# A three-block model on one core: order in the last attention steps and at the forget heads, a second chunk stage begun tile by tile, and changes at the route and its refill

## The chip, the core and the metric

One Trainium2 chip; the kernel runs on one of its cores. TensorE (PE) multiplies matrices into eight PSUM banks, VectorE (DVE) and ScalarE (ACT) read them and work on rows, GpSimd (POOL) takes a few products and the broadcast rows, and SyncE (SP) issues the transfers of all weights. Each engine runs its own instructions in order and waits on semaphores. The metric is the device time in microseconds (us) of one execution.

## What is computed

Two layers of hybrid attention (`first_block`), then one layer of a second model (`second_block`), all in float32, for 256 tokens of width 1024. Cut to what matters here:

```python
# first block, each of 2 layers
h = split_cols((x * (1 + scale) + shift) @ w_in)
o_dsa = attention over the top 64 keys, chosen by an index score
o_fox = softmax(q k / 8 + cum_t - cum_s) v      # cum: running sum of log_sigmoid(forget logit)
o_nsa = gated sum of compressed, selected and window attention
x = layer_norm(ALPHA * x + (1 + gate) * ((mix * silu(gate_cols)) @ w_out))
# second block
streams q, k, v, decays g and weights beta, for the context (s=0) and the latents (s=1)
gdn_chunked: per chunk of 64 tokens, head and direction
    A = strict(kb k^T * decay);  T = (1 + A)^-1;  u = T (v beta);  w = T (kb exp(gcum))
    then a scan over 4 chunks: v_new = u - w state;  o = q state + attn v_new;  state = ...
h = h + gt1 * (concat(chunk_mlp, gdn_out) @ w_out)
aff = softmax(rms_norm(h) ... @ w_router + b_router)
each of 16 experts takes its 32 best tokens: silu(x w_gate) * (x w_up) @ w_down, added back by gate
out = rms_norm(h + gt2 * experts)
```

## The kernel before, in words

**The stream.** All weights pass as 148 units of 2 MB in the order of use (`unit_order`). SyncE issues them one after the other; each waits until the unit that held its place before has been used, by the event of the last product that read it (`slots`, and the loop at L517 to L547). There are 4 places in a ring, and 6 more that come free only when the second block ends with them (the slots of `more` and `pieces`). Of those, the three of `pieces` are filled by two transfers of 1 MB, all else by one of 2 MB. From unit 52 on the units are the experts': four of gate and up, then two of down, for each expert. Unit 54 takes a place that the first products of the second chunk stage have read (`G_mm`), 55 waits for the last state product but one, 56 and 57 for the last mixed rows, 58 and 59 for the output products `y2_mm`, 60 for the last half of the residual (`h_lat`), 61 for the last growth row (`grow_mm`), and 62 for the first expert product (`gu_mm` 0, 0), whose ring slot it refills. 65 waits for the first down product.

**Attention** (`pe_attend`, L932). Eleven pairs of heads pass through a pipeline: scores at step m, transposes of the probabilities of m-2 (`pe_probT`), the product with V of m-3 (`pe_pv`). ACT and DVE turn scores into probabilities and copy the transposes. Between them PE works off products of other kinds. When the pairs are through (steps 11 and 12), the output product's first five chunks are worked, one half of the columns at each step (`pe_y`, ranges 0 to 5), between `pe_pv` and `pe_probT`.

**Forget heads** (`pe_layer`, L990; `v_layer`). After column group 4 PE turns (transposes) block 7, whose rows are H's, then blocks 8 to 10, which are forget heads and need the running sums. DVE finds the top 64 of the first tile in 8 rounds (`v_top`), then copies the running sums (`v_fox_cum`), then H (`v_h` 4), then copies block 7 (`v_turn` 7, four operations), adds the compress offsets (`v_blocks`), copies block 9, ropes q and copies block 11. The second half of the compress product (`pe_cmp1`, bank 3) needs block 11's copy, and behind it stands the product of column group 5 for tile 1.

**Chunk stages** (`pe_chunks`, `v_chunks`, `a_chunks`), s=0 for the context and s=1 for the latents, each of two tiles of 128 tokens with banks 0 to 3 and 4 to 7. DVE spreads g and beta over 512 columns (`v_spread`); PE transposes k and v (`k_mm`, `v_mm`), sums the decays (`R_mm`, `BR_mm`), multiplies k by k and q (`G_mm`). `v_head` copies V with a factor, makes the differences (`diff`), ACT their exponential (`decay`), DVE masks them (`M`) and, for the latents, the attention part; level 0 gives `TT` from `Y`, and `T` from the transposed `Y` (`Y_mm` 0). Five levels follow, with small 64 by 64 products, DVE, ACT and POOL in turn. In each part tile 0 goes before tile 1. The end of a stage makes U and W (`U_mm`, `W_mm`). The context's states are worked between the latents' levels. `pe_recur` is the scan of the latents.

**Route** (`pe_route`, `v_route`, `a_route`). The residual is transposed and multiplied by the router while ACT sums the squares of each tile in one operation of 1024; root, reciprocal, softmax; PE transposes the affinities; two growth rows (`pe_grow`) follow on PE while DVE finds the 32 best tokens of each expert in four rounds of 8; PE transposes the places (`place_mm`) and gathers the first four experts' rows (`pe_gather_first`).

**Experts** (`pe_experts`). For each: gate and up products, transposes, down products, and the add of the last expert's result into banks 0 to 3. The last unit comes in two halves; the four last adds stand behind its second half. `v_final` and `a_final` norm the rows and write them.

## Time and profile before

| | us |
|---|---|
| median of 3 runs | 1230.63 (1230.54 to 1231.61) |
| profiled execution: time | 1233.2 |
| profiled execution: span | 1231.4 |
| PE busy | 1060.6 (86%) |
| DVE busy | 432.9 (35%) |
| ACT busy | 236.2 (19%) |
| mean granted clock of PE | 0.937 |

```profile
PE   5999999999999999999998989899776676666667
DVE  0128645423865536255146764421000000100001
PEclk9999999999999999899998989799887888988879
DMA  9963348443346964014221004899999999999996
GB/s 384 414 244 137 138 145 333 146 156 133 130 148 254 429 263 154 1 69 159 82 104 70 4 30 177 340 427 429 430 428 432 429 428 433 428 430 430 430 430 287
PE 58%; DMA 29%; DVE 6%; issue 3%; ACT 2%; SPq 1%; POOL 0%; DVEq 0%; ACTq 0%; POOLq 0%
```

The first five lines cut the span into 40 slices of 30.8 us: busy tenths of PE and DVE, the clock granted to PE in tenths of full speed, the busy share of the transfer engines and what they moved. The last line is the chain of work that ended last, by engine. Attention is in slices 0 to 14, the streams to 18, the context's chunk stage to 20, the latents' to 23, mixing and route to 25, the experts from there.

### The profile page before, as it was taken

How to read it: one execution, taken by the hardware profiler on the slowest of the kernel's cores; microseconds unless marked ns; L12 is line 12 of the kernel's file. 1: busy time of each engine (PE TensorE's matmuls, PEld its weight loads, DVE VectorE, ACT ScalarE, POOL GpSimd, SP SyncE). 2: the span in 40 equal slices, each digit the busy share in tenths (PEclk: the TensorE clock that was granted, in tenths of full speed). 3: DMA queues.
4: the chain of work that ended last, by engine and by line, in shares of the span. 5: the costliest groups of instructions: out<-in, count | busy, mean ns of one | idle time of the engine just before them, and what ended most of it. 6: DMA issues, size and time to landing. Idle time of an engine off the chain costs nothing.

```text
span 1231.4 us, 17863 instructions
## 1 busy us (share of the span) xinstructions
PE 1060.6 (86%) x7574; PEld 572.8 (47%) x7574; DVE 432.9 (35%) x1026; ACT 236.2 (19%) x584; POOL 54.3 (4%) x69
## 2 busy tenths in 40 slices
PE   5999999999999999999998989899776676666667
PEld 2345764444576447985667875432211111111112
DVE  0128645423865536255146764421000000100001
ACT  0012134111313504434112341210000000000002
POOL 0101000000100000000212310000000000000000
PEclk9999999999999999899998989799887888988879
DMA  9963348443346964014221004899999999999996
GB/s 384 414 244 137 138 145 333 146 156 133 130 148 254 429 263 154 1 69 159 82 104 70 4 30 177 340 427 429 430 428 432 429 428 433 428 430 430 430 430 287
DMA packets 28014, 323.66 MB, mean 263 GB/s; under 512 B 3248, under 2 KB 3376, under 8 KB 5792
## 3 DMA queue, kind: packets, MB, share of 16 engines
q1 hardware_dynamic: 25904, 314.18, 62.2%
q0 software_dynamic: 2032, 8.35, 2.0%
q8 instruction: 60, 0.98, 0.3%
q14 instruction: 18, 0.15, 0.0%
HBM read 321.47 MB, written 1.05 MB: 262 GB/s over the span
## 4 chain that ended last, share of the span: by engine, by line
PE 58%; DMA 29%; DVE 6%; issue 3%; ACT 2%; SPq 1%; POOL 0%; DVEq 0%; ACTq 0%; POOLq 0%
PE banks L638 48%; DMA zuv_to_Kt<-in_stream 16%; DMA ring<-in_stream 7%; DMA scr_qk<-in_stream 6%; PE banks L649 3%; PE banks L2160 1%; PE banks L901 1%; SPq L545 1%; PE banks L887 1%; PE banks L922 1%; PE banks L884 1%; PE banks L788 1%; DVE KC L1237 0%; PE banks L892 0%; DVE scr_qk L2495 0%
## 5 line engine op out<-in xcount | busy, mean ns | idle before, releaser
L638 PE MATMUL banks<-ring,uT 128*128 128x512 f32 (+1 forms) x512 | 224.8, 593 | 6.0 <-DVE uT L1104 2.9
L638 PEld LDWEIGHTS banks<-ring,uT 128*128 128x128 f32 x512 | 95.7, 191 | 119.6 <-issue 114.0
L638 PE MATMUL banks<-scr_qk 64*64 64x64 f32 (+4 forms) x2368 | 116.8, 276 | 23.0 <-DMA scr_qk<-in_stream 18.1
L638 PE MATMUL banks<-ring,scr_qk 128*32 128x512 f32 (+1 forms) x496 | 86.0, 650 | 28.1 <-DMA ring<-in_stream 27.7
L638 PEld LDWEIGHTS banks<-scr_qk 64*64 64x64 f32 (+3 forms) x2368 | 87.0, 138 | 48.1 <-issue 33.7
L638 PE MATMUL banks<-ring,UWK 128*32 128x512 f32 (+1 forms) x336 | 86.1, 788 | 16.1 <-DMA ring<-in_stream 9.1
L2705 DVE SCALAR_TENSOR_TENSOR UWK<-UWK,banks 128x256 f32<-128x256 f32 x16 | 6.7, 421 | 261.4 <-ACT UWK L2972 261.4
L2972 ACT ACTIVATE UWK<-banks 128x256 f32<-128x256 f32 x16 | 6.1, 383 | 359.3 <-PE banks L638 359.3
L638 PE MATMUL banks<-UWK,ring 128*128 128x256 f32 x320 | 72.1, 385 | 0.0
L638 PEld LDWEIGHTS banks<-UWK,ring 128*128 128x128 f32 x320 | 61.7, 194 | 9.4 <-issue 1.0
L2160 PE MATMUL banks<-UWK 128*128 128x512 f32 x128 | 64.9, 632 | 0.0
L638 PEld LDWEIGHTS banks<-ring,scr_qk 128*32 128x32 f32 (+1 forms) x496 | 24.5, 125 | 77.1 <-issue 45.6
L649 PE MATMUL banks<-ring,KC 128*32 128x512 f32 x384 | 49.0, 636 | 12.5 <-DMA ring<-in_stream 12.5
L638 PE MATMUL banks<-uT,ring 128*128 128x256 f32 x256 | 59.2, 392 | 0.0
L638 PEld LDWEIGHTS banks<-ring,UWK 128*32 128x32 f32 (+1 forms) x336 | 26.9, 150 | 60.5 <-issue 48.7
L638 PEld LDWEIGHTS banks<-uT,ring 128*128 128x128 f32 x256 | 50.1, 199 | 7.1
L2713 DVE TENSOR_TENSOR UWK<-banks,grow 128x512 f32<-128x512 f32 x16 | 11.1, 692 | 107.2 <-PE banks L638 107.2
L1605 ACT ACTIVATE probs<-banks,mx 128x128 f32<-128x128 f32 x88 | 36.6, 418 | 42.0 <-DVE mx L1374 37.9
L2160 PEld LDWEIGHTS banks<-UWK 128*128 128x128 f32 x128 | 22.7, 197 | 46.3 <-issue 46.3
L1126 DVE COPY H<-banks 128x512 f32<-128x512 f32 (+1 forms) x12 | 8.2, 681 | 84.8 <-PE banks L638 84.7
L638 PE MATMUL banks<-const,scr_qk 64*64 64x64 f32 (+1 forms) x208 | 15.9, 384 | 22.6 <-DMA misc<-in_stream 20.3
L638 PE MATMUL banks<-Vt_to_O,UWK 128*64 128x128 f32 (+1 forms) x208 | 25.9, 557 | 8.2 <-ACT UWK L2980 4.6
(374 smaller groups left out, 1217.0 us busy)
## 6 DMA issues: line engine op xcount, KB each, us to landing
ring<-in_stream SPq DMA_DIRECT2D x94, 2048.0 KB, 14.2
scr_qk<-in_stream SPq DMA_DIRECT2D x11, 2048.0 KB, 38.8
Vt_to_O<-in_stream SPq DMA_DIRECT2D x11, 2048.0 KB, 38.5
zuv_to_Kt<-in_stream SPq DMA_DIRECT2D x10, 2048.0 KB, 38.9
scr_qk<-in_stream SPq DMA_DIRECT2D x11, 1024.0 KB, 41.3
wide<-in_stream SPq DMA_DIRECT2D x10, 1024.0 KB, 39.0
const<-in_stream SPq DMA_DIRECT2D x10, 1024.0 KB, 39.0
misc<-in_stream SPq DMA_DIRECT2D x10, 1024.0 KB, 39.9
```

Of the source, the lines that this page charges most:

```text
L545: sp.dma_start(held(slot[k]), A["stream"][k, :, :]).then_inc(*tick(f"arrived{slot[k]}", by=16))
L638: return pe.matmul(o, a, b, start=start, stop=stop)
L649: ins = pe.matmul(bank[b][32 * j:32 * j + 32, :], window[:, j * (DCH // 4) + k, lo:lo + 32], w[:, j * (DCH // 4) + k, :], start=(n, k) == ...
L788: ins = pe.transpose(bank[b][0:rows, (2 * m + t) * P:(2 * m + t + 1) * P], f(t), ident)
L884: pe.matmul(bank[b + s][:, 0:P], q[:, 0:P], k[:, 0:P], start=True, stop=False)
L887: pe.matmul(bank[b + s][:, P:384], q[:, P:SEQ], k[:, :], start=False, stop=False)
L901: ins = pe.transpose(bank[4 + s][:, i * P:(i + 1) * P], probs[:, m % 3, s, i * P:(i + 1) * P], ident)
L922: pe.matmul(bank[6][HD * s:HD * s + HD, 0:SEQ], H[:, 0, v:v + HD], probT[:, m % 2, s, 0:SEQ], start=first and kind != "slc", stop=False)
L1126: dve.tensor_copy(H[:, 1, AT[cg]:AT[cg] + WIDTHS[cg]], bank[b][:, 0:WIDTHS[cg]]).then_inc(*drain(b, "h", l, cg, 1))
L1605: ins = act.activation(probs[:, i, s, lo:hi], bank[b + s][:, lo:hi], ACT.Exp, bias=mx[:, i, s, t:t + 1], accum_out=den[:, i, s, t:t + 1])
L2160: ins = pe.matmul(bank[2 * t + h], PgT[:, t, :], ye[:, h, 0:512], start=e == 0, stop=e == EXPERTS - 1)
L2713: dve.tensor_tensor(ye[:, 0, 0:512], bank[4], grow[:, 0:512], ALU.mult).then_inc(*drain(4, "ye", e, 0))
```

## The change

At steps 11 and 12 of attention the partial output product stands before `pe_pv`. In each attention layer the running sums of the forget heads are copied after six of the eight rounds of the top 64, and PE turns blocks 8, 9, 10 before 7. In the latents' chunk stage PE works tile 0's decays, first products and transposes before tile 1's, with k's transposes in bank 2 (6) and not 0 (4); DVE spreads tile 0 between the U and W copies of the context's stage and interleaves the tiles; ACT copies V and loads its exponential ahead. The stream's unit 54 waits for the last V transposes. At the route ACT squares tile 1 by halves, before the second logit copy, and DVE adds the two sums; PE has two products of 512 and 256 columns whose result is not used, each behind a round of the top-k. Unit 62 is filled in two halves, the first when half of the first expert product is done. Of the last adds, one stands before the wait for the last half. The context's stage keeps its order.

```diff
@@ -66,6 +66,7 @@
 ONCE = SPLIT[2]
+PLACES = RING + EXTRA + 1
@@ -193,7 +194,7 @@
         past = seen.setdefault(b, [])
-        parts[b] = parts.get(b, 0) + (2 if b in SPLIT and k < len(order) - 1 else 1)
+        parts[b] = parts.get(b, 0) + (2 if (b in SPLIT or k == first + PLACES) and k < len(order) - 1 else 1)
         use.append(parts[b])
@@ -525,10 +526,13 @@
                     sp.dma_start(par[:, P_FIRST:P_COLS], A["params"][:, P_FIRST:P_COLS]).then_inc(*tick("params_in", "params", 1, by=16))
-                if before[k] is not None:
+                again = units[before[k]] == ("gu_mm", 0, 0) if before[k] is not None else False
+                if again:
+                    sp.wait_ge(*at("gu_half"))
+                elif before[k] is not None:
                     sp.wait_ge(*at(*units[before[k]]))
                 elif slot[k] == RING:
-                    sp.wait_ge(*at("G_mm", 1, 1))
+                    sp.wait_ge(*at("v_mm", 1, 1))
                 elif slot[k] == SPLIT[0]:
@@ -537,8 +541,10 @@
                     sp.wait_ge(*at("mix2", 1, 1))
-                if k == len(units) - 1 or slot[k] in SPLIT:
+                if k == len(units) - 1 or slot[k] in SPLIT or again:
                     for i, half in enumerate(halves(slot[k])):
+                        if again and i:
+                            sp.wait_ge(*at(*units[before[k]]))
                         sem = "arrived_last" if (k, i) == (len(units) - 1, 1) else f"arrived{slot[k]}"
@@ -934,6 +940,12 @@
                     pe_scores(pe, l, m)
+                if m == NPAIR:
+                    w_out += [take(pe)]
+                    pe_y(pe, l, 0, 0, w_out, range(0, 5))
+                if m == NPAIR + 1:
+                    w_out += [take(pe)]
+                    pe_y(pe, l, 0, 1, w_out, range(0, 5))
                 if m >= 3:
@@ -947,12 +959,6 @@
                             pe_mod_rows(pe, n)
-                if m == NPAIR:
-                    w_out += [take(pe)]
-                    pe_y(pe, l, 0, 0, w_out, range(0, 5))
-                if m == NPAIR + 1:
-                    w_out += [take(pe)]
-                    pe_y(pe, l, 0, 1, w_out, range(0, 5))
                 if 2 <= m < NPAIR + 2:
@@ -1011,7 +1017,7 @@
                 if cg == 4:
-                    for n in (7, 8, 9, 10):
+                    for n in (8, 9, 10, 7):
                         pe_turn(pe, l, n)
@@ -1502,8 +1508,9 @@
             v_index(dve, l)
-            v_top(dve, 0, P, TOPK // 8)
+            v_top(dve, 0, P, TOPK // 8 - 2)
             v_fox_cum(dve, l)
+            v_top(dve, 0, P, 2)
             v_h(dve, l, 4)
@@ -1804,50 +1811,72 @@
+        def pe_kv_T(pe, s, t):
+            g = TILES * s + t
+            pe.wait_ge(*at("k_ready", s))
+            for b, lo, event in ((4 * t + (2 if s else 0), 0, "k_mm"), (4 * t + 1, H2, "v_mm")):
+                pe.wait_ge(*free(b))
+                for h in range(H2):
+                    ins = pe.transpose(bank[b][:, h * P:(h + 1) * P], KVT[:, lo + h, g * P:(g + 1) * P], ident)
+                ins.then_inc(*fill(b, event, s, t))
+        def pe_decays(pe, s, t):
...
+        def pe_first_products(pe, s, t):
...
+        def pe_first_Y(pe, s, t):
...
+            if s:
+                for t in range(TILES):
+                    pe_decays(pe, 1, t)
+                    pe_first_products(pe, 1, t)
+                    if t:
+                        pe_first_Y(pe, 1, 0)
+                    pe_kv_T(pe, 1, t)
+                pe_first_Y(pe, 1, 1)
+            else:
+                for t in range(TILES):
+                    pe_kv_T(pe, 0, t)
+                for t in range(TILES):
+                    pe_decays(pe, 0, t)
+                for t in range(TILES):
+                    pe_first_products(pe, 0, t)
             if s == 0:
...
                 pe_zuv(pe, zw, 2, 1, 5)
+                for t in range(TILES):
+                    pe_first_Y(pe, 0, t)
             for n in range(LEVELS):
...
+                for t in range(TILES) if n else ():
                     pe.wait_ge(*free(4 * t + 1))
...
+                    pe.wait_ge(*at("T", s, t, n - 1))
+                    ins = small64(pe, 4 * t + 1, scr[:, t, M_, :], scr[:, t, T_, :], t)
                     ins.then_inc(*fill(4 * t + 1, "Y_mm", s, t, n))
@@ -2071,6 +2100,10 @@
             pe_grow(pe, 1)
+            pe.wait_ge(*at("O", 3, 0))
+            for n, width in ((2, 512), (3, 256)):
+                pe.wait_ge(*at("top", n))
+                mm(pe, bank[6][:, 0:width], ident, resid[:, 0, 0:width], True, True)
             pe.wait_ge(*at("place"))
@@ -2118,6 +2151,8 @@
                                  w[:, :, j * 256:(j + 1) * 256], k == 0, k == DCH - 1)
+                    if (e, i, kk) == (0, 0, 0):
+                        ins.then_inc(*tick("half_used", "gu_half"))
                 ins.then_inc(*fill(6, "gu_mm", e, i))
@@ -2132,6 +2167,15 @@
                 ins.then_inc(*fill(7, "hT_mm", e))
+            def add(e, h, tiles=range(TILES)):
@@ -2142,6 +2186,7 @@
                         if final and h:
+                            add(e, 0, (0,))
                             pe.wait_ge(K.sem("arrived_last"), 16)
@@ -2194,8 +2230,8 @@
                 down(e)
-            for h in range(2):
-                add(EXPERTS - 1, h)
+            add(EXPERTS - 1, 0, (1,))
+            add(EXPERTS - 1, 1)
@@ -2394,52 +2430,78 @@
+                v_diff(dve, s, t)
+            for t in range(TILES):
+                v_first_mask(dve, s, t)
+            v_lat_norm(dve)
+            for t in range(TILES):
+                v_first_TT(dve, s, t)
+            for t in range(TILES):
+                v_first_T(dve, s, t)
+        def v_head_latent(dve):
+            v_diff(dve, 1, 0)
+            v_spread(dve, 1, 1)
+            v_first_mask(dve, 1, 0)
+            v_diff(dve, 1, 1)
+            v_attn(dve, 0)
+            v_first_TT(dve, 1, 0)
+            v_first_mask(dve, 1, 1)
+            v_first_T(dve, 1, 0)
+            v_attn(dve, 1)
+            v_first_TT(dve, 1, 1)
+            v_first_T(dve, 1, 1)
...
+        def v_attn(dve, t):
@@ -2498,22 +2560,22 @@
             if s:
-                for t in range(TILES):
-                    v_spread(dve, 1, t)
-            v_head(dve, s)
-            if s == 0:
-                v_lat_norm(dve)
+                v_head_latent(dve)
+            else:
+                v_head(dve, 0)
             for n in range(LEVELS):
...
                     v_Vnew(dve, 0, n, 1, 0).then_inc(*drain(0, "Vnew", 0, n))
-                if n < LEVELS - 1:
+                if 0 < n < LEVELS - 1:
                     v_level(dve, s, n)
-                else:
+                elif n:
                     for t in range(TILES):
                         dve.wait_ge(*at("Y_mm", s, t, n))
+                        if s:
+                            dve.wait_ge(*at("Vt", 1, t))
                         v_weigh(dve, s, t, AT_, Vt, beta, "bV")
@@ -2541,6 +2603,8 @@
                 dve.tensor_copy(WT[:, t, 4:8, :].rearrange("p i d -> p (i d)"), bank[4 * t + 3][:, :]).then_inc(*drain(4 * t + 3, "W", s, t, 1))
+                if s == t == 0:
+                    v_spread(dve, 1, 0)
@@ -2609,6 +2673,8 @@
             v_fT(dve, 1)
+            dve.wait_ge(*at("ssq_h", 2))
+            dve.tensor_tensor(ssq[:, 1:2], ssq[:, 1:2], ssq[:, 2:3], ALU.add).then_inc(*tick("vector_step", "ssq_sum"))
@@ -2616,9 +2682,9 @@
         def v_route(dve):
-            dve.wait_ge(*at("route_mm"))
             dve.wait_ge(*at("rs_h"))
             inverse(dve, rs2[:, 0:TILES], "rs_row")
+            dve.wait_ge(*at("route_mm"))
             for t in range(TILES):
@@ -2643,7 +2709,7 @@
                 src = w if n else first
-                dve.max(t8[0:EXPERTS, :], src).then_inc(*tick("vector_step"))
+                dve.max(t8[0:EXPERTS, :], src).then_inc(*tick("vector_step", "top", n))
                 dve.wait_ge(*last("vector_step"))
@@ -2852,15 +2918,30 @@
         def a_chunks(act, s):
-            for t in range(TILES):
+            def copy_k(t, b):
                 act.wait_ge(*at("k_mm", s, t))
-                if s:
+                act.activation(Kt[:, t, :, :].rearrange("p h d -> p (h d)"), bank[b][:, :], ACT.Copy).then_inc(*drain(b, "Kt", s, t))
+            def decays(t):
+                act.wait_ge(*at("diff", s, t))
+                act.activation(scr[:, t, M_, :], scr[:, t, M_, :], ACT.Exp).then_inc(*tick("scalar_step", "decay", s, t))
+            if s:
+                act.activation(lowest, C("ones")[:, 0:1], ACT.Exp).then_inc(*tick("scalar_step"))
+                for t in range(TILES):
+                    decays(t)
                     act.wait_ge(*at("KG", 0, t))
                     act.wait_ge(*at("bK", 0, t))
-                act.activation(Kt[:, t, :, :].rearrange("p h d -> p (h d)"), bank[4 * t][:, :], ACT.Copy).then_inc(*drain(4 * t, "Kt", s, t))
-            for t in range(TILES):
-                act.wait_ge(*at("diff", s, t))
-                act.activation(scr[:, t, M_, :], scr[:, t, M_, :], ACT.Exp).then_inc(*tick("scalar_step", "decay", s, t))
+                    copy_k(t, 4 * t + 2)
+                    act.wait_ge(*at("v_mm", 1, t))
+                    act.wait_ge(*at("bV", 0, t))
+                    act.activation(Vt[:, t, :, :].rearrange("p h d -> p (h d)"), bank[4 * t + 1][:, :], ACT.Copy,
+                                   scale=0.5).then_inc(*drain(4 * t + 1, "Vt", 1, t))
+            else:
+                for t in range(TILES):
+                    copy_k(t, 4 * t)
+                for t in range(TILES):
+                    decays(t)
             if s == 0:
@@ -2928,16 +3009,28 @@
         def a_route(act):
-            for t in range(TILES):
+            def square(i, x):
+                act.activation(uwk[:, 0:x.shape[-1]], x, ACT.Square, accum_out=ssq[:, i:i + 1]).then_inc(*tick("scalar_step", "ssq_h", i))
+                act.wait_ge(*last("scalar_step"))
+            def copy(t):
                 b = 2 * t + 1
...
                                ACT.Copy).then_inc(*drain(b, "fT", t, 1))
-                for half in range(2):
-                    act.wait_ge(*at("h_lat", t, half))
-                act.activation(uwk[:, 0:D], resid[:, t, :], ACT.Square, accum_out=ssq[:, t:t + 1]).then_inc(*tick("scalar_step"))
-                act.wait_ge(*last("scalar_step"))
+            copy(0)
+            for half in range(2):
+                act.wait_ge(*at("h_lat", 0, half))
+            square(0, resid[:, 0, :])
+            act.wait_ge(*at("h_lat", 1, 0))
+            square(1, resid[:, 1, 0:512])
+            act.wait_ge(*at("h_lat", 1, 1))
+            square(2, resid[:, 1, 512:D])
+            act.wait_ge(*at("ssq_sum"))
             root(act, rs2[:, 0:TILES], ssq[:, 0:TILES], D, "rs_h")
+            copy(1)
             act.activation(lowest, C("ones")[:, 0:1], ACT.Exp).then_inc(*tick("scalar_step"))
...
```

## Rows read from the trace of the kernel before

**Rows 1.** Stretches: length, busy us of each engine, PE's clock, DMA share, GB/s.
```profile
785.00:794.00 9.00, 6.19 (x27) 4.16 (x30) 5.14 (x14) 0.91 (x2) 0.00 (x0) 0.52 1.01 425
794.00:796.00 2.00, 2.00 (x20) 1.09 (x12) 1.10 (x2) 0.00 (x0) 0.00 (x0) 1.00 0.15 57
796.00:798.00 2.00, 2.00 (x19) 0.45 (x17) 0.00 (x0) 0.91 (x2) 0.00 (x0) 1.00 1.01 254
798.00:800.00 2.00, 2.00 (x24) 1.28 (x24) 0.80 (x2) 0.00 (x0) 0.00 (x0) 1.00 0.94 401
...
800.00:900.00 100.00, 86.30 (x594) 28.81 (x590) 13.96 (x26) 8.43 (x19) 0.53 (x1) 0.91 1.01 429
```
**Rows 2.** Timeline of SyncE's issues: start, us, what, [idle before and releaser].
```profile
770.46 4.64 SPq L545 DMA_DIRECT2D ring<-in_stream  x2
...
795.16 3.26 SPq L545 DMA_DIRECT2D ring<-in_stream  x2
...
809.62 0.33 SPq L545 DMA_DIRECT2D Vt_to_O<-in_stream  x1
```
**Rows 3.** Timeline of PE, end of attention in layer 0.
```profile
210.00 0.65 PE L922 MATMUL banks<-H 128*64 128x256 f32 x4 [0.74 <-DVE H L1396]
...
210.80 4.56 PE L638 MATMUL banks<-ring,uT 128*128 128x512 f32 x10
```
**Rows 4.** Timeline of PE, end of attention in layer 1.
```profile
433.30 0.65 PE L922 MATMUL banks<-H 128*64 128x256 f32 x4 [0.74 <-DVE H L1396]
...
434.74 4.56 PE L638 MATMUL banks<-ring,uT 128*128 128x512 f32 x10 [0.57 <-DMA ring<-in_stream]
```
**Rows 5.** Timeline of PE, forget heads and compress, layer 0, then layer 1.
```profile
110.07 0.63 PE L788 MATMUL banks<-const,H 128*128 128x128 f32 x4 [1.08 <-DVE wide L1207]
110.53 1.47 PE L788 MATMUL banks<-const,wide 128*66 128x128 f32 x12
...
121.61 2.05 PE L638 MATMUL banks<-probs,w 128*64 128x30 f32 x32 [0.29 <-DVE TB L1237]
...
123.59 6.28 PE L638 MATMUL banks<-ring,uT 128*128 128x448 f32 x16
...
322.98 0.63 PE L788 MATMUL banks<-const,H 128*128 128x128 f32 x4 [0.90 <-issue]
...
336.62 7.80 PE L638 MATMUL banks<-ring,uT 128*128 128x448 f32 x16
```
**Rows 6.** One stretch as in rows 1, the head of the second chunk stage.
```profile
654.50:670.20 15.70, 12.09 (x175) 9.41 (x175) 14.42 (x24) 3.74 (x5) 1.75 (x2) 0.92 0.37 133
```
**Rows 7.** Timeline of PE and VectorE, end of the first chunk stage, second's head.
```profile
650.61 0.69 DVE L2541 COPY UWK<-banks 128x512 f32<-128x512 f32 x1 [2.83 <-PE banks L638]
...
653.82 3.57 PE L1816 MATMUL banks<-const,scr_qk 128*128 128x128 f32 x16
...
669.96 2.19 PE L638 MATMUL banks<-scr_qk 64*64 64x64 f32 x64 [0.96 <-POOL scr_qk L566]
```
**Rows 8.** Timeline of ScalarE and PE, the route.
```profile
777.94 1.05 ACT L2938 ACTIVATE UWK<-resid 128x1024 f32<-128x1024 f32 x1
...
782.20 3.62 PE L638 MATMUL banks<-misc,const 128*128 128x512 f32 x4
...
787.86 0.39 PE L2077 MATMUL banks<-const,UWK 16*128 16x16 f32 x2 [2.03 <-DVE UWK L2661]
...
789.03 3.75 PE L638 MATMUL banks<-UWK 128*128 128x128 f32 x16 [0.78 <-DVE UWK L2665]
...
792.71 2.38 PE L638 MATMUL banks<-ring,scr_qk 128*32 128x512 f32 x16
...
795.02 1.16 PE L638 MATMUL banks<-UWK 128*128 128x128 f32 x8
```
**Rows 9.** Timeline of PE, VectorE and ScalarE, the tail.
```profile
1219.78 0.69 DVE L2713 TENSOR_TENSOR UWK<-banks,grow 128x512 f32<-128x512 f32 x1 [5.19 <-PE banks L638]
...
1221.02 1.06 PE L638 MATMUL banks<-zuv_to_Kt,UWK 128*32 128x512 f32 x8 [1.38 <-DMA zuv_to_Kt<-in_stream]
...
1222.02 3.70 PE L2160 MATMUL banks<-UWK 128*128 128x512 f32 x8
...
1223.18 0.60 ACT L2993 ACTIVATE UWK<-banks 128x512 f32<-128x512 f32 x1 [5.68 <-PE banks L2160]
```

More of the change, by code:

```diff
@@ L2134, in hidden_T @@
                 ins.then_inc(*fill(7, "hT_mm", e))
+            def add(e, h, tiles=range(TILES)):
+                pe.wait_ge(*at("ye", e, h))
+                for t in tiles:
+                    if e == 0:
+                        pe.wait_ge(*free(2 * t + h))
+                    ins = pe.matmul(bank[2 * t + h], PgT[:, t, :], ye[:, h, 0:512], start=e == 0, stop=e == EXPERTS - 1)
+                    if e == EXPERTS - 1:
+                        ins.then_inc(*tick("moe_done", "moe_mm", e, t, h))
             def down(e):
@@ L2500, in v_chunks @@
             if s:
-                for t in range(TILES):
-                    v_spread(dve, 1, t)
-            v_head(dve, s)
-            if s == 0:
-                v_lat_norm(dve)
+                v_head_latent(dve)
+            else:
+                v_head(dve, 0)
             for n in range(LEVELS):
```

145 lines of the change are left out of this document (62 added, 83 removed).

## The prediction

> **What bounds the kernel now.** I read the page's slices first: moved bytes sit near 430 GB/s from slice 26 to the end, while TensorE (PE) goes slack there; before that PE is nearly always busy and the transfers come in bursts. The chain of waits says the same: PE until 865 us, weight transfers from there to 1221 us, then a short tail. So the last part is set by bytes. The table of stretches fixes where that begins [rows 1]: 429 GB/s over 800 to 900 us, 425 over 785 to 794, but 57, 254 and 401 GB/s in the three stretches of 2 us from 794 to 800. After that no hole is left. Against 427 GB/s the dip lost (2*370 + 2*173 + 2*26)/427 = 2.67 us. SyncE's own queue names it [rows 2]: the refill of the slot of the first expert product is issued at 795.16, when that product is done, and its bytes flow 0.9 us later, the queue having run dry at 794.27. The batch before it starts at 770.46 and flows without a gap (with 0.5 MB of broadcast rows). Two things can make the kernel shorter, then: PE's work before 770 us done earlier moves everything behind it, one for one; and the dip of 2.67 us can be closed. Beyond the dip only the tail is left.
>
> **Attention, last steps.** In layer 0 the PV product of pair 8, and again that of pair 9, waits 0.74 us for a copy of the transposed probabilities, with 4.5 us of output product queued behind it (one of the two stands in [rows 3]). The change puts the output product first; it reads chunks that pairs up to 6 have made, its bank was read by the exponentials of pair 10 before it begins, and it covers both waits: 2*0.74 = 1.5 us gained. Nothing that I see takes their place, since the next transposes then find their bank free. In layer 1 the same two waits stand there, but the output product itself begins at 434.74 because its weights have only just arrived [rows 4]. With the new order the PV product (0.8 us) can't run in front of that arrival any more: 0.8 lost there, 0.74 gained at the next pair. I take 0 (bounds -0.9 and 0.7). The arrival is itself at the end of a stretch limited by bytes, but that stretch was opened by a PE product, so it moves with what comes before.
>
> **Forget heads.** The running sums are copied before the last two rounds of the top-k, so PE can turn heads 8 to 10 at once, where it idles 1.08 us now and then turns block 7 first [rows 5]. PE gains up to 1.2 us at that place. But the next wait is not PE's own: the first compress product of the second half waits for VectorE at 121.61, with only 0.29 us of slack, and VectorE's row of work from block 7's copy to there is unbroken. Block 7 now comes fourth: three turns of 0.44 us (1.31 from start to start) behind a product ending at 108.98 put it at 110.14 instead of 110.07; in layer 1, where the product ends at 322.07, at 323.23 instead of 322.98 [rows 5]. So VectorE's chain starts 0.07 and 0.25 us later and PE gets its gain back as a wait: 0.3 us lost in all (bounds: 0.8 lost, 0.2 gained).
>
> **Second chunk stage.** VectorE is the engine PE waits for here. Its work from the first spread to the last T takes 15.6 us for 22 operations, 0.71 from one to the next (24 in the stretch of [rows 6], which cuts one more at either end), and the first product of level 1 starts at 669.96 [rows 7]. The change leaves 18 of them between the end of the products of the first stage and the same point: the two V copies go to ScalarE, which is busy 3.74 us of the 15.7 [rows 6], and the two spreads of tile 0 go into VectorE's wait of 2.83 us before 650.61 [rows 7]. That is 4*0.71 = 2.8 us less. Against it, its first operation now waits for the decay product of tile 0: PE is free at 653.82 [rows 7], and such a product takes 1.81 us at the half clock (two in 3.62, [rows 8]); the transposes that stand there now run at that clock, with 3.57 us for 16 records, so VectorE starts at about 655.65 and not 654.5: 1.1 lost. PE's part by tiles (decays, first products, first Y, transposes) runs beside it; I walked it through and only the last Y product is tight. Sum: 2.8 - 1.1 = 1.7 us gained. At the full clock the first wait would be 0.9 shorter: 2.6. If ScalarE's or PE's order adds a wait per tile: 1.0. The held slot 4 is filled some 1.5 us later than now (it waits for the last V transposes); SyncE's next issue is not before 735 us, so nothing stands behind it. ScalarE's early exponential only moves a table load into its idle time.
>
> **Route.** Now ScalarE squares the whole of tile 1 (1.05 us, plus its 0.19 us read) after the last residual half, and the root follows [rows 8]. By halves only 0.60 + 0.19 us stand behind it, as for the squares of 512 at the end [rows 9], but a VectorE add comes in, and the copy for the logits stands behind the root, 0.2 us later than now. The exponential comes some 0.3 us earlier. From there the chain is VectorE's top-k. The idle products stand on PE behind the growth rows, which run at half clock: two in 3.62 us, to 785.8 [rows 8]. The 512-wide one then ends at 787.3 to 787.5 and the 256-wide one at 788.2; the place transposes, now at 787.86, would wait for that: 0.7 us of the way lost. If they bring the clock up, what follows is cheaper: the first gather takes 3.75 us for 16 records, where 8 records take 1.16 at the full clock (1.4 saved), and the first expert product 2.38 against 1.92 (0.4 saved) [rows 8]. So PE's route is between 0.4 longer and 2.2 shorter. Neither end is shown by a row: the clock fell within a microsecond of PE's last logit product and rose only in the middle of the gathers. I take the middle, 0.9 shorter.
>
> **Halved refill.** The first half can be issued after 8 of the 16 records, 1.0 us earlier. With 0.9 from the route the first bytes are asked for at 793.3, just when the queue runs dry: the dip is closed, 2.67. The next gate is the refill behind the first down product, issued at 809.62 [rows 2]. Three units of 4.91 us (2.1 MB at 427 GB/s) from 794.27 end at 809.0; the issue would be at 808.7 and flow 0.9 later: 0.6 of the gain goes into a new small hole there. I take 2.0 us for route and refill together (bounds 0.5 and 2.67). With the route unchanged, the half alone would bring 0.9.
>
> The row of 785 to 794 us holds the other half-size transfers (units in two pieces of 1 MB) at 425 GB/s [rows 1]. The Trainium skill (DMA: Bandwidth & Descriptors, "Bandwidth", "Measured") has 1 MB transfers at 341 GB/s and 6.15 us, 78% of the peak. By that rule the halved unit would cost 1.2 us more than the whole one and the dip would stay; the row, where pieces overlap in the queue, speaks against it.
>
> **Tail.** One of the four last adds now stands before the wait for the last half. VectorE has scaled its input at 1220.47, the half lands at 1221.02; the add (0.92, eight records in 3.70) ends at 1221.4 [rows 9]. So the last down product starts 0.4 later, and three adds are left instead of four: 0.92 - 0.4 = 0.5 us gained (bounds 0 and 0.9).
>
> **Sum.** 1.5 + 0 - 0.3 + 1.7 + 2.0 + 0.5 = 5.4 us. The profiled execution has a span of 1231.4 and a time of 1233.2; it would go to 1227.8. The median of the three timed runs is 1230.63, 2.6 below the profiled one, so I expect 1225.2. What a measurement of this kernel tells from no change is about 0.2%, 2.5 us.
>
> **Rivals.**
> (a) The route stays at half clock and the idle products only stand in the way of the place transposes: route and refill bring 0.5. Gain 3.9, time 1226.7. For it: the clock fell with PE just stopped. Against: they fill most of what was empty. 0.20.
> (b) All goes well: route at full clock, dip closed without the second hole (2.67), chunk stage 2.6, tail 0.5. Gain 1.5 - 0.3 + 2.6 + 2.67 + 0.5 = 7.0, time 1223.6. 0.17.
> (c) PE's waits move and the clock falls where it does not now. A block product costs 7.80 us against 6.28 when the half clock hits it [rows 5]: 1.5 each. PE now idles 1.4 us before the compress product in both layers and 2.2 us in one piece before layer 1's output weights arrive. Two or three such stretches leave a gain of 0.9 to 2.4, time about 1229. 0.11.
> (d) Slower: the same, in the levels of the second chunk stage (670 to 703 us, PE all but saturated at the full clock now). One us at half clock there costs 0.5, so the change loses from 11 us of added half clock on; 16 us of it would make 8.0 - 5.4 = 2.6 us more than now, time 1233.2. For it: the stage's larger products ran at half clock while PE was busy. Against: the first stage's levels and these kept the full clock throughout. 0.04.
> (e) Pieces of 1 MB don't overlap and flow at the 254 GB/s of 796 to 798 us: the unit takes 8.3 us and not 4.9, and route and refill bring nothing. Gain 3.4, time 1227.2. The row of 785 to 794 us is against. 0.03. The skill's page above would make it a milder case of this.
> The forecast itself has 0.45, its own range 1224.1 to 1226.3.
>
> **How the numbers follow.** Faster by over 0.2% (below 1228.2): the forecast, (a), (b), (e) and a part of (c), 0.86 less some doubt that terms carry through: 0.83. Within 0.2%: 0.12. Slower: 0.05. The range 1221.8 to 1228.2 takes in (a), (b), (e) and the bounds of the terms, and leaves out most of (c) and (d).
>
> **What would show it.** The waits of 0.74 us ahead of the PV products gone in layer 0, the start of layer 1's block products 1.4 us earlier; the compress product waiting over 1 us for VectorE; the first level product of the second stage some 3 us earlier in all (the chunk part 1.7 of it); the first half refill issued some 5 us before 795.16, no slice below 400 GB/s around it; granted clock at 1.00 in the gathers. It would be wrong if the batch now issued at 770.46 does not come 2.5 to 3.5 us earlier, or if the transfers of the experts, once running, take another time than now.

## The result, and the profile after

The changed kernel is slower: over 20 runs each its median is 1238.41 us (1229.67 to 1244.62) against 1233.39 us for the kernel before (1223.22 to 1239.17), a ratio of 1.0041 with a 95% interval of 1.0024 to 1.0058. 5.4 us less was forecast (1225.2 us); 5 us more came. The forecast's starting point was low besides: the median of its three runs (1230.63) lies 2.5 us below the mean of 183 executions of the same kernel, measured later for the most part (1233.17). The profiled execution of the changed kernel took 1244.62 us with a span of 1242.8, the slowest of its 20, so its trace shows where such a kernel loses time, and only the medians show how much.

The page after: busy time, slices of the granted clock and of the moved bytes.

```profile
PE 1074.2 (86%) x7578; PEld 581.5 (47%) x7578; DVE 431.9 (35%) x1025; ACT 238.1 (19%) x589; POOL 54.1 (4%) x69
...
PEclk9999899999899999799998979899889888888899
...
GB/s 384 415 233 136 135 142 332 163 162 126 109 167 251 428 238 153 1 68 136 70 134 72 4 1 204 313 409 430 430 428 431 429 427 432 430 430 431 429 429 274
```

From slice 27 on bytes flow at 427 to 432 GB/s, as before (slice 26: 409 for 427), so nearly all of the loss lies in front of it. SyncE's timeline after, with the same columns as [rows 2]:

```profile
781.67 4.64 SPq L551 DMA_DIRECT2D ring<-in_stream  x2
...
803.77 1.19 SPq L549 DMA_DIRECT2D ring<-in_stream  x2
807.58 0.33 SPq L551 DMA_DIRECT2D ring<-in_stream  x1
810.52 0.33 SPq L551 DMA_DIRECT2D scr_qk<-in_stream  x1
819.11 0.33 SPq L551 DMA_DIRECT2D Vt_to_O<-in_stream  x1
820.82 0.33 SPq L551 DMA_DIRECT2D zuv_to_Kt<-in_stream  x1
822.54 2.04 SPq L551 DMA_DIRECT2D ring<-in_stream  x2
```

The batch that started at 770.46 [rows 2] starts 11.2 us later; it was forecast 2.5 to 3.5 earlier. Behind it the distance shrinks to 9.5 us at 819.11 (before: 809.62). One stretch of 20 to 770 us tells what made the difference, first the kernel before, then the changed one (length, busy us and instructions of PE, PEld, DVE, ACT, POOL; clock; DMA share; GB/s):

```profile
20.00:770.00 750.00, 718.69 (x5442) 465.88 (x5440) 373.26 (x904) 199.99 (x502) 52.58 (x62) 0.98 0.43 167
```

```profile
20.00:770.00 750.00, 722.04 (x5406) 470.17 (x5406) 369.41 (x898) 200.21 (x504) 52.41 (x62) 0.95 0.43 165
```

PE is as busy, at a clock of 0.95 and not 0.98. Finer stretches show it at the half clock (1.2 GHz) for 34 us before and for 68 after. Where PE is busy throughout, 3.4 us of it cost about 1.67: where one of two traces of the same program (e5 and e12, both below) has such a stretch and the other has not, they move apart by 1.7 us.

The places, in the changed kernel. PE's timeline at the compress products of layer 0, of layer 1, and at the output product of layer 1:

```profile
117.18 2.05 PE L644 MATMUL banks<-probs,w 128*64 128x30 f32 x32
120.83 3.62 PE L644 MATMUL banks<-probs,w 128*64 128x30 f32 x32 [1.60 <-DVE TB L1243]
...
331.48 2.05 PE L644 MATMUL banks<-probs,w 128*64 128x30 f32 x32
335.13 3.53 PE L644 MATMUL banks<-probs,w 128*64 128x30 f32 x32 [1.60 <-DVE TB L1243]
...
437.58 6.25 PE L644 MATMUL banks<-ring,uT 128*128 128x512 f32 x10 [2.12 <-DMA ring<-in_stream]
```

Each new wait is there as foreseen (1.60 us for VectorE; 2.12 in one piece for the weights), and the very instruction behind it runs at half speed: 3.62 for 2.05, 6.25 for 4.56 [rows 4]. In layer 0 the clock fell at 120.22, still inside the wait. Further on, PE and VectorE at the head of the second chunk stage:

```profile
662.86 3.68 PE L644 MATMUL banks<-scr_qk,const 128*128 128x512 f32 x4
...
674.77 1.15 PE L644 MATMUL banks<-const,scr_qk 64*64 64x64 f32 x32 [1.12 <-DVE scr_qk L2481]
...
677.16 2.08 PE L644 MATMUL banks<-scr_qk 64*64 64x64 f32 x64
```

```profile
664.93 0.69 DVE L2460 TENSOR_TENSOR scr_qk<-banks,lows 128x512 f32<-128x512 f32 x1 [1.27 <-PE banks L644]
```

From the end of the first stage (662.86, was 653.82) to the first level product (677.16, was 669.96 [rows 7]) it takes 14.3 us instead of 16.14: 1.8 less. Then, around the last products of the stage, the stretch of 690 to 740 us in the changed kernel:

```profile
690.00:740.00 50.00, 45.69 (x879) 43.15 (x877) 29.15 (x44) 13.71 (x33) 12.53 (x10) 0.83 0.01 2
```

0.17 below full over 50 us is 17 us at half clock; the kernel before had 0.93, 7 us.

### The profile page after: what moved, and what is told of

Same layout as the page of the kernel before. It is cut to its first block, busy times and chain, and to the rows that moved or that the text cites. A ratio compares the mean times of both kernels' runs of the same rounds, so it can differ in the third digit from the quotient of the medians.

```text
span 1242.8 us, 17886 instructions
## 1 busy us (share of the span) xinstructions
PE 1074.2 (86%) x7578; PEld 581.5 (47%) x7578; DVE 431.9 (35%) x1025; ACT 238.1 (19%) x589; POOL 54.1 (4%) x69
## 4 chain that ended last, share of the span: by engine, by line
PE 59%; DMA 32%; DVE 5%; issue 2%; ACT 1%; SPq 1%; POOL 0%; DVEq 0%; ACTq 0%; POOLq 0%
PE banks L644 48%; DMA ring<-in_stream 23%; DMA zuv_to_Kt<-in_stream 8%; PE banks L655 3%; PE banks L907 1%; PE banks L893 1%; PE banks L928 1%; PE banks L2176 1%; SPq L551 1%; PE banks L794 1%; PE banks L890 1%; DVE KC L1243 0%; PE banks L898 0%; DVE scr_qk L2557 0%; PE banks L931 0%
## 5 line engine op out<-in xcount | busy, mean ns | idle before, releaser
L644 PE MATMUL banks<-ring,uT 128*128 128x512 f32 (+1 forms) x512 | 227.7, 599 | 7.2 <-DVE uT L1110 2.9
L644 PEld LDWEIGHTS banks<-scr_qk 64*64 64x64 f32 (+3 forms) x2368 | 90.1, 140 | 46.9 <-issue 31.2
L644 PE MATMUL banks<-const,scr_qk 64*64 64x64 f32 (+1 forms) x208 | 18.8, 442 | 22.3 <-DMA misc<-in_stream 21.2
```

The source lines that it names most:

```text
L644: return pe.matmul(o, a, b, start=start, stop=stop)
```

## Experiments

All ran in five groups, 12 executions of each kernel, with the kernel before run beside them in every group (35 executions, 23 in the last). The table gives the parts of the change that a kernel holds (F forget heads, A0 and A1 output product first in layer 0 and in layer 1, C chunk stage, R route, refill and tail), its ratio with interval, and from its one trace the us at half clock around the compress products (115 to 135 and 330 to 350), at 690 to 740, and in all up to 770.

```
kernel            parts           ratio  interval        115  330  690  all
before            -               -      -               0.0  3.4  6.8  34
changed           F A0 A1 C R     1.0041 1.0024-1.0058   6.8  6.8 17.1  68
e1                F               1.0011 0.9988-1.0035   6.8  3.4 10.2  55
e2                A0 A1           1.0010 0.9982-1.0038   0.0  0.0  0.0  27
e3                C R             1.0015 0.9989-1.0040   3.4  0.0 17.1  51
e4  filled        F A0 A1 C R     1.0000 0.9980-1.0020   0.0  0.0 10.2  34
e5                C               1.0049 1.0027-1.0071   0.0  3.4 10.2  41
e6                R               1.0001 0.9975-1.0026   0.0  6.8  6.8  48
e7                A0 C R          1.0004 0.9974-1.0034   0.0  0.0 10.2  41
e8  e7, filled    A0 C R          0.9992 0.9965-1.0019   0.0  0.0 10.2  38
e9                F A0 A1 R       1.0043 1.0017-1.0070   6.8  6.8 10.2  61
e10               A0 R            0.9997 0.9971-1.0022   0.0  0.0 10.2  34
e11 filled        F A0 A1 R       0.9980 0.9945-1.0015   0.0  0.0  0.0  27
e12 as e5         C               1.0020 0.9991-1.0050   3.4  0.0 17.1  51
e13 head filled   -               1.0022 1.0007-1.0038   3.4  3.4  0.0  31
e14 as before     -               1.0005 0.9984-1.0025   3.4  3.4  3.4  34
e15 PV filled     A0 R            0.9989 0.9964-1.0013   0.0  0.0 10.2  38
e16 as e11        F A0 A1 R       1.0005 0.9977-1.0033   6.8  3.4 10.2  51
e17               A1              1.0014 0.9987-1.0042   6.8  0.0  3.4  41
e18               F A0 C R        1.0034 1.0006-1.0062   3.4  3.4 17.1  55
```

**First parts alone, and the waits filled (e1 to e4).** e1 is the kernel before with

```
-                    for n in (7, 8, 9, 10):
+                    for n in (8, 9, 10, 7):
-            v_top(dve, 0, P, TOPK // 8)
+            v_top(dve, 0, P, TOPK // 8 - 2)
             v_fox_cum(dve, l)
+            v_top(dve, 0, P, 2)
```

> The kernel before with the forget heads' new order alone (turns 8, 9, 10, 7 on TensorE; running sums before the last two rounds of the top-k on VectorE). Theory A (the clock falls where PE is left waiting): PE's wait between the two compress products grows from 0.29 to about 1.6 us in both layers, a half clock stretch begins right behind it in at least one of them, and the kernel is 1 to 4 us slower than before. Theory B (the loss sits in the later parts): 0.3 us slower, as priced. Theory C (half clock stretches fall anywhere): 0.3 us slower, no stretch tied to the wait.

> The kernel before with the output product ahead of the PV product in the last steps of both layers, alone. Theory A: 1.5 us gained in layer 0; in layer 1 the wait for the output weights becomes one piece of 2 us or more, and the half clock that follows it costs 1.5 us or so: between 1 us faster and 1 us slower. Theories B and C: 1.5 us faster, the output product of layer 1 at the full clock.

> The changed kernel with forget heads and attention order put back as before: second chunk stage, route, halved refill and tail add alone. Theory A: the whole loss comes from the front, so this is 3 to 5 us faster than before (4.2 as priced), with the first half refill issued at once when the queue runs dry. Theory B: 2 to 6 us slower than before, with longer half clock stretches from 650 us on. Theory C: 4.2 us faster.

e4 is the changed kernel with this, and the like with two products of 512 ahead of the `take` of layer 1's output weights:

```
                 pe.wait_ge(*free(2 + v))
+                if v == 0:
+                    for width in (512, 256):
+                        mm(pe, bank[2][:, 0:width], ident, resid[:, 0, 0:width], True, True)
```

> The changed kernel with idle products of a 128 x 512 and a 128 x 256 operand ahead of the first compress product in both layers, and two of 128 x 512 ahead of the wait for layer 1's output weights (their results are overwritten). Theory A: PE no longer idles for over 1 us at these three places, the half clock stretches behind them go, and the kernel is 2 to 4 us faster than the changed one. Theories B and C: as the changed one, 0.4% slower than before, or a little more where an idle product stands in the way.

None of e1 to e3 is clear of no change by itself. e1 lies at the low end of theory A's 1 to 4 us (1.1 by the means, standard error 1.2), with A's half clock stretch behind the wait in its trace, in layer 0:

```profile
121.69 3.39 PE L638 MATMUL banks<-probs,w 128*64 128x30 f32 x32 [1.61 <-DVE TB L1237]
```

e2 (1.2 us slower by the ratio) is nearer to A's end of its range than to the 1.5 us faster of B and C, which its interval still holds. e3 contradicts its part of A: it should have been 3 to 5 us faster and isn't. e4 bears A out: the same work as the changed kernel plus idle products is 7.2 us faster than it in the mean (standard error 1.1), 5.1 by the ratios, against 2 to 4 expected. Ratio and means of one kernel can lie 2 us apart (the ratio has e4 at no change, the means at 1.9 us faster than before), so neither is read more finely than that. Its timeline at the compress products of layer 0:

```profile
117.71 1.46 PE L644 MATMUL banks<-resid,const 128*128 128x512 f32 x4
119.10 2.05 PE L644 MATMUL banks<-probs,w 128*64 128x30 f32 x32
121.45 2.05 PE L644 MATMUL banks<-probs,w 128*64 128x30 f32 x32 [0.30 <-DVE TB L1250]
```

The idle products (first row) make the first compress product 1.4 us later, the wait before the second one is 0.30 us, and it takes 2.05 again.

**Which of the late parts (e5 to e8).** e5 has the chunk stage's functions of the change alone, e6 the rest of the late part, e7 is e3 with the output product first where l is 0.

> The kernel before with the second chunk stage's new order alone. The work itself: 1.9 us gained between the end of the first stage and the first level product of the second, as in the runs so far. Theory A (what is gained is work, what is lost is half clock, and the later parts draw more of it only by chance): 1.9 us faster in the mean. Theory B (the new order makes the clock fall longer behind the levels, 17 us of half clock around 717 to 735 us as in both runs with this order unfilled, against 0 to 10 in those without): 2 to 3 us slower in the mean, and over 10 us of half clock between 705 and 735 us again.

> The kernel before with the route by halves, the idle products, the halved refill and the tail add alone. The dip in the transfers at 794 to 799 us closes (2.6 us), but the next refill, which waits for the first down product, leaves a hole of 1.4 us some 20 us later; the adds at the end bring 0.3. Theory A: 1.2 to 1.5 us faster in the mean. The prediction's terms: 2.5 us faster. A rival, that the clock gained in the route is taken back later: no change.

> The changed kernel with the forget heads' order put back and the output product first in layer 0 alone. No wait of 1.6 or 2.1 us arises in front of 440 us, so by theory A the work sums to 1.7 (attention, layer 0) + 1.9 (chunk stage) + 1.2 (route, refill, tail): 4.8 us faster than before in the mean. Theory B: 0 to 2 us faster.

> e7 with idle products as well ahead of the last large products of both chunk stages (384 wide, in a wait of 0.81 us) and ahead of the recurrences (512 and 128 wide, in a wait of 1.3 us). If the clock falls behind the 64 x 64 products because of these waits: less half clock than in e7 at 640 to 660 and 705 to 735 us and 1 to 4 us faster than e7. If it falls because of the products themselves: as e7.

e5 is slower clear of its interval, by more than theory B's 2 to 3 us; B's second sign (over 10 us of half clock at 705 to 735) is just met, 10.2. e6 gives no change, the rival's outcome, though 1.2 to 1.5 lie within its interval. e7 is a little beyond B's end. e8's fills leave the half clock at 640 to 660 and 705 to 735 us as it was. In the first stage they closed the wait of 0.81; in the second they closed the one of 1.3, which lies behind the fall, but the one of 0.81 only shrank to 0.54. So the second stage's stretches don't come from the wait of 1.3 us, and hardly from that of 0.81.

**The change without the chunk stage (e9 to e12).**

> The changed kernel with the second chunk stage in its old order. Theory B (the chunk stage's new order costs more than the 1.9 us it gains, by longer half clock behind it): 2 to 5 us faster than the changed kernel, that is 0 to 3 us slower than before. Theory A alone (all loss from the waits in front of 440 us, the chunk stage a pure gain): 1.9 us slower than the changed kernel, 7 us slower than before.

> e7 (forget heads as before, output product first in layer 0 alone) with the old chunk stage: attention of layer 0, route, refill and tail are left. Theory B: 1.7 + 1.2 = 2.9 us faster than before, and 2 to 4 us faster than e7. Theory A alone: 1 us faster than before and 1.9 us slower than e7.

> e4 (the changed kernel with idle products in the front waits) with the old chunk stage. Theory B: 1 to 3 us faster than e4, 3 to 5 faster than before. Theory A alone: 1.9 us slower than e4, no faster than before.

> e5 once more, on the chip and in the rounds of e9 to e11. Theory B: 3 to 6 us slower than before again, over 6.8 us of half clock between 705 and 735 us. If e5 was chance: within 2 us of before.

e9 fell between the two (1.0043, 4.3 us by the means): a large part of the loss is made in the front. e10 is 2.1 us faster than before by the means and 0.4 by the ratio, where B asked for 2.9 and A for 1. e9 and e11 differ by the front fills alone; their stretch of 115 to 135 us:

```profile
115.00:135.00 20.00, 18.39 (x112) 12.91 (x111) 8.96 (x26) 3.59 (x7) 0.00 (x0) 0.83 0.12 32
```

```profile
115.00:135.00 20.00, 19.68 (x133) 14.38 (x132) 11.93 (x35) 3.63 (x7) 0.00 (x0) 1.00 0.25 88
```

Clock 0.83 and 1.00, 112 against 133 product records in the same 20 us. e12 repeats e5's sign with less size (2.4 us by the means where e5 had 5.0). Around the last products of the stage e12 shows what the new order goes with, e14 (the kernel before again) what the old does:

```profile
708.00 14.21 PE L638 MATMUL banks<-scr_qk 64*128 64x64 f32 x96 [0.81 <-DVE scr_qk L2543]
...
723.51 1.98 PE L638 MATMUL banks<-Vt_to_O,UWK 128*64 128x128 f32 x16 [1.30 <-DVE UWK L2591]
```

```profile
708.80 8.60 PE L638 MATMUL banks<-scr_qk 64*128 64x64 f32 x96 [0.81 <-DVE scr_qk L2495]
...
718.70 1.09 PE L638 MATMUL banks<-Vt_to_O,UWK 128*64 128x128 f32 x16 [1.30 <-DVE UWK L2543]
```

The same 96 records behind the same wait take 14.21 and 8.60 us. These two traces are far apart; the first trace of the kernel before has 10.22.

**Why the chunk stage costs, and a search for a better version (e13 to e16).** e13 puts idle products into the three waits at the head of the stage in the old order:

```
                     pe.wait_ge(*free(4 * t + 1))
+                    for width in {(1, 0, 0): (512, 256), (1, 0, 1): (384,), (1, 1, 0): (384,)}.get((s, n, t), ()):
+                        mm(pe, bank[4 * t + 1][:, 0:width], ident, C("level")[:, 0:width], True, True)
```

> The kernel before, chunk stage in its old order, with idle products of 128 rows (512 and 256, 384, and 384 wide) in the three waits of PE at the head of the second chunk stage (1.46, 0.90 and 0.96 us at 663 to 670 us), which the new order closes too. Theory D (a PE without pauses at the head of the stage draws more half clock behind the levels; the new order costs by that): over 10 us of half clock between 705 and 735 us and 2 to 4 us slower than before. If the cost of the new order has another cause: within 1 us of before and 0 to 10 us of half clock there.

> The kernel before itself, run as if it were a change: a second trace of it, and what the comparison makes of no change. All theories: a ratio of 1.000 within its interval; between 705 and 735 us 0 to 10 us of half clock as in the six other traces with the old chunk order.

> e10 (output product first in layer 0, route, refill, tail; forget heads, layer 1 and chunk stage as before) with idle products of 512 and 384 columns in the wait of 1.81 us ahead of the first PV product of both layers, behind which a half clock stretch began in five of thirteen traces. Theory A: that stretch goes, 0.5 to 1 us faster than e10 and 3 to 4 us faster than before. Else: as e10.

> e11 once more (the changed kernel with idle products in the front waits and the old chunk stage): 2 to 4 us faster than before if its first result holds.

Theory D is half contradicted: e13's trace has no half clock at all between 690 and 740 us, but its time is 2.7 us slower by the ratio, clear of its interval and of D's size (0.3 by the means, without one execution of 2796 us). The idle products also left waits of 0.42 and 0.52 us at the head, so D is not settled. e14, the same program as before, comes out at 1.0005. e15 and e16 are not faster than before beyond their intervals, and e15's trace has no better time than e10's; e16 takes back e11's promise, and in its trace the clock fell at the compress products (6.8 us) though the wait was 0.31. No version tried beats the kernel before beyond doubt.

**Layer 1's order (e17, e18).**

> The kernel before with the output product first in layer 1 alone. A least squares fit over the runs so far gives this part +4.4 us (standard error 1.0) and the same edit in layer 0 -2.7. Theory A (the wait for the output weights gathers into one piece of 2.1 us, behind it the half clock in most executions): 0.5 of work and 1.7 of half clock, 2 to 4 us slower than before. As the prediction priced it: no change.

> The changed kernel with the output product first in layer 0 alone. Theory A: 2 to 4 us faster than the changed kernel (1.001 to 1.003 of before). As priced: as the changed kernel, 1.004.

Both come out near the middle (1.7 us slower than before by the ratio; 0.9 faster than the changed kernel): neither is decided alone. A least squares fit of the mean times of all kernels but e13 (execution counts as weights, one execution of 1335 us, e15's, left out) puts all together: F +2.8 us, A0 -1.8, A1 +2.7, C +2.1, R -0.1, and F with A1 filled -0.3. The standard errors are 0.5 for C and 0.7 to 0.9 for the others, and about a quarter more by how far the kernels scatter around the fit. C is less even than one number says: alone it cost 4.7 and 2.8 us (e5, e12), on top of all the rest 0.6 (the changed kernel against e9, both against the 183). The sum of the parts for the changed kernel is 5.7; it was 5.4 slower than the mean of 183 executions of the kernel before (1233.17).

A trace shows the clock of one execution, but the mean granted clock was read in each timed execution too. Turned into us at half clock over the whole span, the same fit over 386 executions gives F +6.8 us (standard error 2.3), A1 +5.4 (2.3), C +9.1 (1.7), R -5.7 (2.4), A0 0.1 (2.6), and F with A1 filled +1.7 (2.7). The three parts that cost time are the three that add half clock, and with the front waits filled what F and A1 add is gone within the error.

## Why the prediction was wrong

**The work went as priced, nearly term by term.** Attention, layer 0: the waits of 0.74 are gone; the traces gain 1.7 us there and the fit has -1.8, for the 1.5 forecast. PE after, against [rows 3]:

```profile
210.49 0.88 PE L907 MATMUL banks<-const,probs 128*128 128x128 f32 x6
211.20 4.46 PE L644 MATMUL banks<-ring,uT 128*128 128x512 f32 x10
215.59 0.65 PE L928 MATMUL banks<-H 128*64 128x256 f32 x4
```

Forget heads: in e1's trace the kernel falls back by 3.4 us over both layers, with 6.8 us more of half clock (3.3); 0.1 is left for the work, forecast 0.3. Chunk stage: 1.8 to 2.0 us less in the traces that hold it, forecast 1.7. The dip at 794 to 799 us closed: the packet records with 182 and with 180 MB of the queue left lie 11.30 and 8.70 us behind those of the kernel before, 2.6 gained for 2.67. The second hole, priced at 0.6, is larger. Stretches of the changed kernel:

```profile
814.00:818.00 4.00, 4.00 (x33) 1.72 (x36) 0.68 (x1) 1.88 (x4) 0.00 (x0) 1.00 1.01 434
818.00:822.00 4.00, 4.00 (x44) 1.30 (x40) 1.38 (x2) 0.00 (x0) 0.00 (x0) 1.00 1.00 352
822.00:826.00 4.00, 4.00 (x30) 1.60 (x19) 0.28 (x1) 0.00 (x0) 0.00 (x0) 1.00 0.89 348
```

4*(427-352)/427 + 4*(427-348)/427 = 1.4 us; from 0.3 to 2.3 by the packet records of the twelve traces that hold this part, 1.1 in the mean. Its refill was not late: issued at 819.11, 807.9 in the old time, earlier than the 808.7 counted on. That term counted as a hole only the time with an empty queue; the likeliest reading, not shown by a run of its own, is that the rate stays low while that one unit is alone in it, until those of 820.82 and 822.54 follow. The route itself became no shorter up to the gathers:

```profile
796.60 1.48 PE L644 MATMUL banks<-resid,const 128*128 128x512 f32 x4
799.37 0.29 PE L2110 MATMUL banks<-const,UWK 16*128 16x16 f32 x2 [1.28 <-DVE UWK L2727]
800.44 2.02 PE L644 MATMUL banks<-UWK 128*128 128x128 f32 x16 [0.78 <-DVE UWK L2731]
802.65 1.92 PE L644 MATMUL banks<-ring,scr_qk 128*32 128x512 f32 x16 [0.19 <-issue]
```

The place transposes (second row) are at 799.37, 11.5 behind 787.86 [rows 8] where the batch is 11.2 behind: not earlier. The whole gain is in the clock of what follows (2.02 for 3.75, 1.92 for 2.38 [rows 8]), 2.2 us where the prediction's upper case had 1.8; the clock had risen at 796.1, ahead of the idle products here. That they raise it is not shown; that the part as a whole does is: from 770 to 802 us the twelve traces that hold it have 3.4 or 6.8 us of half clock, the eight without it 10.2 or 13.7. (In the kernel before it rose at 793.7, in the first expert product, and not in the middle of the gathers.) The tail gained 0.3 and not 0.5: the last down product starts 3.01 us after the one before, was 2.44 (1218.58 to 1221.02 [rows 9]), and the rest of the span takes 9.5 us for 10.4. From the issue of the batch (770.46 before) to the end, the twelve traces with route, refill and tail take 459.8 us in the mean and the eight without 461.4: 1.6 us gained of the 2.5 priced (1.0 if e1 and e5, whose last packets came late, are left out). The fit's -0.1 is too coarse to show it.

```profile
1230.28 1.07 PE L644 MATMUL banks<-zuv_to_Kt,UWK 128*32 128x512 f32 x8 [0.36 <-DMA zuv_to_Kt<-in_stream]
...
1232.23 1.13 PE L2176 MATMUL banks<-UWK 128*128 128x512 f32 x2 [0.88 <-DVE UWK L2779]
1233.29 1.07 PE L644 MATMUL banks<-zuv_to_Kt,UWK 128*32 128x512 f32 x8
```

In the profiled execution that makes: +9.0 us at the end of the first chunk stage, -1.8 for the head of the second, +4.0 to the end of the recurrences, -2.6 for the dip, +1.8 for the second hole and what drifts behind it, +1.3 for last packets that come late, -0.3 for the tail: 11.4.

**What failed: three terms priced the work and the wait and put the clock at nothing.** They are the forget heads' 0.3 lost, layer 1's 0 and the chunk stage's 1.7 gained. For the first two this is rival (c), taken for small. The prediction named the mechanism (waits move, the clock falls where it did not), named the two places, gave it 0.11 and let it leave a gain. It failed in two ways. The chance: it asked whether a fall would happen, from one trace; it is a matter of how often. In the four traces with F unfilled the compress products lie in 6.8, 6.8, 6.8 and 3.4 us of half clock in layer 0 (mean 6.0) and in 5.1 in layer 1; in the other sixteen in 1.7 and 1.5. 7.9 us more, at 1.67 for 3.4, is 3.9 us, and the fit has F at +2.8 where 0.3 of work was priced. Behind a wait of 1.6 us the clock fell within 2.6 us of the second compress product's start, or in the wait, in eight of eight cases; behind one of 0.3 in 12 of 32. The size: 1.5 us for a fall stands for one stretch of 3.4 us; in layer 0 it lasted 6.8 in three of the four.

**Rival (d) was near, with its place wrong.** The levels (670 to 703 us) kept the full clock in every trace. Behind them, in the products of 64 rows that end the stage and in the recurrences, the eight traces with the new order hold 17.1, 17.1, 10.2, 10.2, 10.2, 10.2, 17.1 and 17.1 us of half clock between 690 and 740, the twelve with the old one 0 to 10.2, 6.0 in the mean. 7.7 us more, at the 0.40 per us that the traces give there, is 3.1 us: more than the 1.9 that the order saves. So the term "1.7 gained" is a loss of 2.1 by the fit. Why the new order draws it is open. It isn't the wait of 1.3 us (e8), and e13's trace, though not its time, speaks against the missing pauses at the head. In the traces with 17.1 the fall comes 2.2 to 2.6 us after the start of those products, where it comes later (2.9 to 4.0) the stretch is 3.4 and then 3.4 or 6.8. With the new order it came after 2.2 to 3.2 us in all eight traces; with the old after 2.9 to 4.0 in seven, after 11.0 in two and not at all in three. What sets that moment was not tried. A1 is the third: its work was priced at 0, and its 2.7 us are less well located. The half clock behind the weights' arrival stands in two of the seven traces that hold it (two of the four unfilled ones), 3.4 us each, which is at most 0.9 us in the mean; that A1 adds 5.4 us of half clock per execution is shown by the clock of the timed executions; where the rest of it falls is not.

## What to carry to other kernels

When an order is changed for a microsecond, look first at the waits of TensorE that it makes longer: here work that was saved term by term nearly as computed was lost about twice over while the clock was lower. One trace is one draw of where the clock falls; sort terms into work (the same in every trace) and clock (count it over several), and give the second its own range before adding. Where a wait can't be avoided, idle products in a bank that is free took most of this loss back here; leaving the order alone did as well.

## What the runs showed of the hardware

- Over the 20 traces, of 191 pauses of TensorE of 1 us or more between 25 and 790 us that began at the full clock, a half clock stretch began in the pause or up to 0.6 us behind it in 36; of 216 pauses of 0.6 to 1 us, in one; of 175 of 0.3 to 0.6 us, in none. But these are 37 of 183 stretches: the others, at 150, 365 and 505 us for instance, begin in the midst of work.
- Executions of one kernel differ: the kernel before took 1223 to 1254 us over 183, standard deviation 4.1. Differences of 3 us need more than twelve runs a side.
- In some traces the last unit's packets land up to 2.3 us behind the bulk (e1, e5). A 16 KB load of the instruction queue stands 25 to 31 us before the end of all twenty traces, so it does not tell them apart. Left open.
